# Keys and queries of an attention step transposed by VectorE and over DRAM instead of by TensorE

## What is computed

```python
z = h @ w_in
q, k, v, u, ga, gc = jnp.split(z, list(np.cumsum(IN_SPLITS)[:-1]), axis=-1)
o = moba_attention(to_heads(q), to_heads(k), to_heads(v))      # 16 heads of 128 channels
y_attn = o.transpose(0, 2, 1, 3).reshape(B, S, ATTN_WIDTH) @ w_attn_out
y_conv = conformer_conv(u, conv_dw, conv_db, conv_ln_g, conv_ln_b, w_conv_out)
merged = jax.nn.sigmoid(ga) * y_attn + jax.nn.sigmoid(gc) * y_conv
return merged @ w_out
```

## Time and profile before

| | us |
|---|---|
| median of 3 runs | 2117.32 (2117.18 to 2117.36) |
| the profiled execution | 2117.16 |
| its span in the trace | 2115.3 |
| TensorE busy | 2102.1 (99%) |
| VectorE busy | 1868.6 (88%) |
| ScalarE busy | 1406.2 (66%) |
| GpSimd busy | 194.2 (9%) |

### The profile page before, as it was taken

How to read it: one execution, slowest core, us unless ns; L and a number is a source line. 1 busy time by engine, 2 the same in 40 slices (tenths; PEclk the granted TensorE clock), 3 DMA queues, 4 the chain that set the end, 5 groups by cost and what they waited for, 6 DMA issues and landing times.

```text
span 2115.3 us, 23794 instructions
## 1 busy us (share of the span) xinstructions
PE 2102.1 (99%) x9420; PEld 1740.6 (82%) x9420; DVE 1868.6 (88%) x1404; ACT 1406.2 (66%) x1321; POOL 194.2 (9%) x305
## 2 busy tenths in 40 slices
PE   9999999999999999999999999999999999999998
PEld 7888888888888888888888888888888888888886
DVE  8899999999997889999899986659899999999996
ACT  6677777778775547666676435435677777777773
POOL 0111111100110000000000000000111111110110
PEclk9999999999999999999999999999999999999999
DMA  9688888898886759787888656755688888898883
GB/s 359 238 285 274 266 268 269 293 308 277 288 276 237 274 154 316 251 261 224 273 266 251 232 189 231 259 187 199 237 289 262 276 262 275 290 308 276 288 276 123
DMA packets 89709, 548.26 MB, mean 259 GB/s; under 512 B 12416, under 2 KB 12800, under 8 KB 32512
## 3 DMA queue, kind: packets, MB, share of 16 engines
q1 hardware_dynamic: 68544, 437.69, 54.5%
q0 software_dynamic: 21056, 109.07, 24.5%
HBM read 529.93 MB, written 16.78 MB: 258 GB/s over the span
## 4 chain that ended last, share of the span: by engine, by line
PE 99%; DMA 0%; DVE 0%; SPq 0%; ACT 0%; issue 0%; DVEq 0%
PE acc L2194 16%; PE acc L2196 16%; PE acc L2195 16%; PE tb L2194 12%; PE tb L2196 12%; PE tb L2195 12%; PE acc L2132 3%; PE acc L2134 3%; PE acc L2133 3%; PE tb L2180 1%; DMA g_raw<-in_groups 0%; PE tb L2475 0%; PE tb L2491 0%; PE tb L2492 0%; PE tb L2474 0%; DVE res L2035 0%
## 5 line engine op out<-in xcount | busy, mean ns | idle before, releaser
L1326 DVE TENSOR_TENSOR g_lo<-g_raw,g_hi 128x2048 fp32r<-128x2048 f32 x506 | 1147.3, 2285 | 136.5 <-ACT g_hi L804 136.1
L804 ACT ACTIVATE g_hi<-g_raw 128x2048 fp32r<-128x2048 f32 x506 | 964.7, 1916 | 343.3 <-DVE g_raw L1334 105.4
L2194 PE MATMUL acc<-g_hi,xF_hi 128*128 128x512 f32 x1216 | 477.9, 393 | 1.9 <-DVE g_lo L1653 1.3
L2196 PE MATMUL acc<-g_hi,xF_lo 128*128 128x512 f32 x1216 | 473.7, 390 | 0.0
L2195 PE MATMUL acc<-g_lo,xF_hi 128*128 128x512 f32 x1216 | 473.2, 389 | 0.0
L2194 PE MATMUL tb<-g_hi,xF_hi 128*128 128x512 f32 x760 | 297.1, 391 | 0.0
L2196 PE MATMUL tb<-g_hi,xF_lo 128*128 128x512 f32 x760 | 295.9, 389 | 0.0
L2195 PE MATMUL tb<-g_lo,xF_hi 128*128 128x512 f32 x760 | 295.7, 389 | 0.0
L1334 DVE TENSOR_TENSOR g_raw<-g_raw,g_raw 128x2048 f32<-128x2048 f32 x120 | 274.3, 2286 | 1.4
L2194 PEld LDWEIGHTS acc<-g_hi,xF_hi 128*128 128x128 f32 x1216 | 228.3, 188 | 50.3 <-DVE g_lo L1653 2.6
L2196 PEld LDWEIGHTS acc<-g_hi,xF_lo 128*128 128x128 f32 x1216 | 228.3, 188 | 48.2
(11 more groups left out here) (169 smaller groups left out, 2243.5 us busy)
## 6 DMA issues: line engine op xcount, KB each, us to landing
g_raw<-in_groups SPq DMA_DIRECT2D x356, 1024.0 KB, 7.0
g_raw<-in_groups POOLq DMA_DIRECT2D x80, 1024.0 KB, 8.3
raw<-in_stream SPq DMA_DIRECT2D x80, 512.0 KB, 4.7
bounce<-h_sq POOLq DMA_DIRECT2D x40, 256.0 KB, 5.0
h_in<-bounce POOLq DMA_DIRECT2D x160, 64.0 KB, 2.8
ln_gb<-in_ln SPq DMA_DIRECT2D x6, 1024.0 KB, 6.9
g_raw<-in_groups SPq DMA_DIRECT2D x6, 512.0 KB, 9.1
res<-in_x_rows SPq DMA_DIRECT2D x1, 2048.0 KB, 16.0
```

Of the source, the lines that this page charges most:

```text
L804: act.activation(g_hi[:, n % RING], source[:], ACT.Copy).then_inc(g_hi_ready, 1)
L1326: dve.tensor_tensor(g_lo[:, n % RING], source[:], f32(g_hi[:, n % RING]), ALU.subtract).then_inc(g_lo_ready, 1)
L2194: pe.matmul(bank, x_hi_ap, g_hi[:, n % RING, blk], start=begin, stop=False, skip_group_check=True)
L2196: return pe.matmul(bank, x_lo_ap, g_hi[:, n % RING, blk], start=False, stop=end, skip_group_check=True)
```

## The change

1. **Keys.** VectorE transposes `k_sb` in squares of 32 x 32 into `kT` (`keys_squared`, behind P1b's g_lo), GpSimd's queue writes `kT` to DRAM (`squares_out`), and ScalarE's own queue reads it back into `kT` in four pieces (`heads_in`), in its order ahead of P5a's split.
2. **Queries.** The same through `q_sq` and `q_bounce` (VectorE behind Q1's g_lo, ScalarE's reads ahead of P6a's split), and then ScalarE copies `q_sq` to `qT` behind P6a's split.
3. `turn_k`, `turn_q` and `heads_of` go. The **scores** of pair 0 stand behind P5b instead of Q2, those of pair 1 behind P6a instead of P5b. A head has three matmuls of 128 columns instead of one of 128 and one of 256, since `kT` holds the two halves of rows apart.
4. **Taps.** Ten counts per block: 0, 0, 0, 0, 2, 2, 3, 3, 3, 3 in the blocks with heads (16 as before; block 4 had 23), and 8 or 6 per gate group instead of 7 or 5.
5. **The first chunk.** 10 warm-up matmuls instead of 12; for each part of the first weights the matmuls with g_hi come first and wait for g_hi only, those with g_lo last.
6. **The first block** of the first network: the sum T3 is made by an accumulating DMA on GpSimd's queue (`t3_first`), and two `factor_lo` stand behind T1 instead of before the block.
7. `stats` lies elsewhere in SBUF, and the scratch for GpSimd's DMAs is 2048 instead of 1024.

```diff
-WARM = 12
+WARM = 10
-HALF_SUMS = ("T1", "T3", "T2", "T4")
+HALF_SUMS = (("T1", "T2", "T4"), ("T1", "T3", "T2", "T4"))
-BLOCK_TAPS = ((1, 3), (1, 3), (1, 3), (1, 3), (2, 3), (2, 1))
+HEAD_TAPS = (0, 0, 0, 0, 2, 2, 3, 3, 3, 3)
+BLOCK_TAPS = ((3, 3, 1, 1, 3, 1, 1, 1, 1, 1), *([HEAD_TAPS] * NG), (1, 1, 2, 2, 1, 2, 2, 2, 2, 2))
...
+    k_bounce = nc.dram_tensor("k_bounce", (QD, STEP, QD, TT, BLK, STEP), F32, kind="Internal").ap()
-        kT = mix("kT", [P, HG, T])
+        kT = mix("kT", [P, QD, TT, BLK, STEP])
+        q_sq = place("q_sq", [P, QD, TT, BLK, STEP], at=pr_at)
...
+            def heads_in(g, sent, dst, dram, loaded_all):
+                act.wait_ge(sent, 16 * (g + 1))
+                for c in range(QD):
+                    act.dma_start(dst[STEP * c:STEP * (c + 1)].rearrange("p a t b n -> p a (t b n)"),
+                                  dram[:, :, c].rearrange("a p t b n -> p a (t b n)")).then_inc(loaded_all, 16)
             def queries_turned(g):
+                act.wait_ge(q_loaded, 16 * QD * (g + 1))
                 if g:
                     act.wait_ge(o_stored, 16 * g)
-                heads_of(qT, g, 2)
+                for t in range(TT):
+                    act.activation(qT[:, :, t * P:(t + 1) * P].rearrange("p b (a n) -> p a b n", a=QD), q_sq[:, :, t],
+                                   ACT.Copy).then_inc(qT_ready, 1)
...
+            def square(dst, src, squared_one):
+                dve.transpose(dst.rearrange("p c b n -> p b c n"),
+                              src.rearrange("p (b c n) -> p b c n", b=BLK, c=QD)).then_inc(squared_one, 1)
...
+            def squares_out(g, squared_one, squares, dram, sent):
+                pool.wait_ge(squared_one, TT * (g + 1))
+                pool.dma_start(dram.rearrange("a p c t b n -> (a p) (c t b n)"),
+                               squares.rearrange("p c t b n -> p (c t b n)")).then_inc(sent, 16)
             def mixing_sums(g):
                 f = "mix"
+                if 0 < g <= NG:
+                    squares_out(g - 1, k_squared, kT[:], k_bounce, k_sent)
                 pool.wait_ge(g_lo_ready, lo_count(G.at[f, g, "P1b"]))
                 add_from_hbm(f, g, "qb", "rb", t1b_ready)
+                if 0 < g <= NG:
+                    squares_out(g - 1, q_squared, q_sq[:], q_bounce, q_sent)
...
+            pool.wait_ge(t_ready, G.sum_no[0, 1, "T1"])
+            add_from_hbm(0, 1, "ra", "ua", t3_first)
             round_trips(0)
...
                 for h in (2 * pair, 2 * pair + 1):
-                    pe.matmul(tb[:, h % 2, 0:P], qT[:, h, 0:P], kT[:, h, 0:P], start=True, stop=True)
-                    pe.matmul(tb[:, h % 2, P:SC], qT[:, h, P:T], kT[:, h, :], start=True, stop=True).then_inc(tr_full, 1)
+                    pe.matmul(tb[:, h % 2, 0:P], qT[:, h, 0:P], kT[:, :, 0, h], start=True, stop=True)
+                    pe.matmul(tb[:, h % 2, P:2 * P], qT[:, h, P:T], kT[:, :, 0, h], start=True, stop=True)
+                    pe.matmul(tb[:, h % 2, 2 * P:SC], qT[:, h, P:T], kT[:, :, 1, h], start=True,
+                              stop=True).then_inc(tr_full, 1)
```

More of the change, by code:

```diff
@@ L475, in build @@
         conv_step = sem("conv_step")
-        qk_ready = sem("qk_ready")
+        k_squared = sem("k_squared")
+        q_squared = sem("q_squared")
+        k_sent = sem("k_sent")
+        q_sent = sem("q_sent")
+        kT_loaded = sem("kT_loaded")
+        q_loaded = sem("q_loaded")
+        qT_ready = sem("qT_ready")
         s_ready = sem("s_ready")
@@ L1147, in mixing_block @@
                 if heads:
+                    heads_in(g - 1, q_sent, q_sq[:], q_bounce, q_loaded)
+                split_sum(f, g, "P6a", "qa", "T2a")
+                if heads:
                     queries_turned(g - 1)
-                split_sum(f, g, "P6a", "qa", "T2a")
                 split_loaded(f, g, "P3a", "ua")
@@ L1820, in mixing_block @@
                     conv_value(1)
-                taps(some)
+                if heads:
+                    queries_squared(g - 1)
+                taps(counts[0])
                 lo_group(f, g, "Q2", "Q2")
@@ L2253, in first_chunk @@
                     p = g // 2
-                    pe.wait_ge(part_lo, h + 1)
+                    pe.wait_ge(part_hi, h + 1)
+                    if h in (0, 4, 6):
+                        pe.wait_ge(x_hi, (0, 4, 6).index(h) + 1)
+                    for t in range(TT):
+                        for blk in range(first, last):
+                            high_only(banks[g % 2][t], piece(p, t)[0][:, blk], g, blk, p == 0 and blk == 0)
                     if h in (0, 4, 6):
```

123 lines of the change are left out of this document (66 added, 57 removed).

## The result

The changed kernel takes **2145.18 us** (median of 4 runs, 2143.3 to 2147.28) against 2117.27 for the kernel before beside it: ratio **1.0132**, 95% interval 1.0119 to 1.0144. It is 28 us slower, where 2110.1 (2108.0 to 2114.5) was forecast. Its profiled execution took 2146.07 us for a span of 2143.8.

The account below looks back on a forecast made before the run. TensorE, busy 99% of the span, was taken as the bound; 2117.16 - 1.28 (start) - 6.96 (transposes) + 1.2 (VectorE waits) = 2110.1 us, with a range of 2108.0 to 2114.5 for 8 in 10.

Parts of the forecast that it names:

- The way of the queries: Head blocks, queries through DRAM: qT ready at B + 16.5 to 20.5, wanted by TensorE at B + 21.8, so no wait.
- source of delay: Head blocks, DMA load: the squares add 2.1 MB per block, 31 GB/s, to 267 GB/s at a DMA share of 0.92.
- Rival (b): Head blocks: queries come late, ready at B + 27.3, a 5.5 us wait in each block, 2130.9 us; chance 0.08.
- Start, 1.28: Kernel start, fifth part of the first weights: matmuls begin at 12.35 instead of 13.63 us, a gain of 1.28 us.
- rival (c): First block: the start's gain is lost, VectorE late or P7 held by its DMA, 2111.4 us; chance 0.08.
- Transposes, 6.96: Blocks 1 to 4: turn_k and turn_q leave TensorE, eight pieces of 0.87 us, a gain of 6.96 us.
- Scores, 0: Scores in the head blocks: two 128-column matmuls instead of one of 256, operand in runs of 32 columns, cost 0.
- Rival (d): Scores: the moving operand lying in runs costs 10.5 us more, 2120.6 us; chance 0.03.
- VectorE, 1.2 us at P3b: Head blocks, pair 1's scores to P3b's g_lo: TensorE waits 0.3 us in each of four blocks, 1.2 us.
- Rival (a): Head blocks: VectorE becomes the bound, a block taking 68.1 instead of 66.75 us, time 2114.3 us; chance 0.13.
- Gates, 0: Gate groups: g_lo and eight taps take VectorE 5.5 us of TensorE's 5.44, entered over 4 us ahead: cost 0.
- What queues behind these waits: ScalarE in the head blocks: splits of P5a, P6a and P3a held by transfer waits, all covered by 2 us or more.

Follow-up runs that it names:

- first experiment: Kernel before with only the changed start (10 warm-ups, split first products, later factor_lo, T3 by accumulating DMA): 2116.13 us, ratio 0.9994.
- last run: Eighth experiment's kernel with seven convolution taps put back from the gate groups into block 4: 2112.3 us, ratio 0.9976.
- ninth run: Third experiment's kernel with both pairs of scores, and the steps that follow them, one product group later: 2136.07 us.
- fifth experiment: Third experiment's kernel with only the DRAM layout changed, so the one read DMA moves 1 KB rows instead of 4 KB: 2142.76 us.
- fourth experiment: Changed kernel, narrow rows kept, with GpSimd holding the sum T3b and those behind it until the query read lands: 2124.41 us, ratio 1.0031.
- sixth: Third experiment's kernel with the query write issued on ScalarE's queue behind P5a's split instead of GpSimd's: 2148.17 us.
- seventh: Sixth experiment's kernel with GpSimd also holding back T3b and what follows until the query read lands: 2129.36 us.
- third experiment: Changed kernel with the DRAM layout turned: four writes of 32 partitions in 1 KB pieces, one read with 4 KB rows: 2134.84 us, ratio 1.0085.
- second experiment: Changed kernel without the DMAs writing and reading the squares through DRAM, so scores are not the reference's: 2111.62 us, ratio 0.9971.
- eighth: Third experiment's kernel with only the keys going through DRAM and the queries turned on TensorE as before: 2114.14 us, ratio 0.9983.

## Why the prediction was wrong

**The step that failed is "The way of the queries"**: first its term for the query read, 3.5 us, and with it two terms that were given no time.

- *The read.* "64 KB took 2.8 us; I take 3.5 for 128 KB", with 7.0 as the far end. It took 6.3 to 9.6 us, and 17.8 in block 4. The 2.8 us of the earlier trace rows was a median over the whole kernel. With T3b held back the query read took 3 to 4 us, so 3.5 was its price with next to nothing else in flight; it was not the price in the first 25 us of a head block. It was the read and not the write: the query write landed at B + 13.6 to 15.8, at the late end of the forecast's B + 12 to 15, and with 3.5 us for the read qT would have been in time in three blocks and 0.3 us late in block 2. As it was, qT ended the wait in all four.
- *The keys.* I followed only their write ("lands by B + 2.7"; it landed at B + 3.3) and never costed their read, since 15 us seemed ample. It was the longest transfer, 18.4 to 19.2 us and 24.9 in block 4, and came after the scores were due in every block. It was hidden behind the later queries, and would have been the next wait.
- *Load as a "source of delay".* It was named and given no time. The 0.92 of the earlier trace rows is block 4's mean, and in the stretch in which the trip of block 2 must be done the share was lower still. What was missing is the trip's own engine time, added to that share. The page's part 3 for 897 to 920 before (B - 2.2 to B + 20.8) and for 901 to 926 after (B - 1.7 to B + 23.3), two windows with nearly the same sums and loads:

```profile
q0 software_dynamic: 305, 2.24, 54.2%
q1 hardware_dynamic: 288, 2.10, 22.2%
```

```profile
q0 software_dynamic: 576, 3.15, 55.4%
q1 hardware_dynamic: 288, 2.10, 21.3%
q10 hardware_dynamic: 1127, 1.03, 17.1%
```

Before: 76.4% of 23 us, 17.6 us of all 16 engines. After: 94% of 25 us, 23.5 us. So the trip costs some 6 us of every engine (an estimate from these rows), in a stretch that had 5 to 6 free and in which each transfer waits for another. In block 4 the same stretch was full already before: the share over 1034.4 to 1057.4 was 1.01 (such a share adds up packet times and can come out just above 1), against 0.79 over 899.24 to 922.24 in block 2. The trip had no room there, and the wait was 12.8 us.

**Rival (b) was the right mechanism.** It had 0.08. It had qT ready at B + 27.3, with reads of 7.0 us; in block 2 it was ready at B + 25.9, with reads of 6.3 to 7.3. It gave 5.5 us in each block, 2130.9. Blocks 1 to 3 waited about 4 each; what it lacked is block 4 (12.8) and the half clock behind every wait, 10.01 us in all. Its fault was the chance: the sum went by the kernel-wide median of the reads. The Trainium skill's rule that I cited (DMA: Bandwidth & Descriptors, "Issuing engines are not separate DMA queues") is borne out by the runs: ScalarE's query reads slowed with what GpSimd had in flight, from 3 to 4 us to 6 to 18. I had let it move only the query's read to 7.0 us.

**The other steps.**

- *Start, 1.28.* Right: the fifth part began at 12.19 instead of 13.63, and 1.39 us of it was left at the first head block. The first experiment shows that it differs between executions. No wait at u1, P5 or P7; rival (c) did not come.
- *Transposes, 6.96.* Right: 7.12.
- *Scores, 0.* Right: at full clock two heads take six matmuls of 0.22 us. Rival (d) fell.
- *VectorE, 1.2 us at P3b.* It cost nothing: 267.77 us of block and as much of busy TensorE without the trip. Rival (a) fell.
- *Gates, 0.* Wrong by 1.7 us. VectorE entered the gate groups ahead, as said, but left them late for sig_a. I looked whether the groups themselves were met, not at what stands behind them. In the profiled execution without the trip the stretch behind the blocks was 4.2 us longer than before (1021.79 against 1017.61), with 2.3 us of wait for sig_a and a granted clock of 0.79 just behind it (1224 to 1232). The last run took it back.
- *What queues behind these waits.* "All covered, by 2 us or more" rested on the query read. The ninth run shows the price: P3a's split stood behind it.

The sum without the failed step and without the 1.2 us that VectorE did not need, 2108.9, stands against 2111.62 of the kernel without the trip: the gates and the start that varies are the likely rest of 2.7 us, not told apart by a run.

What stays open: how the engines share themselves out between the queues. The fifth experiment shows a narrow read that is late while each of its packets costs no more than alone (elsewhere up to 68 ns of an engine were seen, with and without load), because few bytes go with each. Taking turns packet by packet with the long rows of the other queues (theory A) fits that, and so do the nearly equal packet counts of the three queues, but nothing here shows the turns themselves. Whether one queue serves its transfers strictly in order (theory C) stays open too. Nor was a trip tried on SyncE's queue.

## What to carry to other kernels

A transfer put on a timeline is priced with the DMA share and the queues of its own stretch plus what it adds itself, not with a median over the kernel. Where that stretch has 5 us of free engines in 25, a trip that needs 6 made something late in every order that was tried, and reordering only chose what. Cost every leg, also the one with ample time, and what stands behind each waiting instruction. Where several conditions release one instruction, compare the end of each with its start; the chain in the profile can name one that had long been met. Add to each wait of TensorE what its clock loses behind it: here 2.0 to 2.8 us a wait, for waits of 2.7 to 12.8 us. Taking half of the trip, the half that fits, beat both kernels.

## What the runs showed of the hardware

- A read of 512 KB took 18.8 us in 1 KB rows and 10.4 in 4 KB rows, with everything else alike, while the DMA share was 1.01 and 1.00. With next to nothing else in flight the query read took 3.0 to 4.0 us in narrow rows (medians of the four blocks, fourth experiment) and 3.1 to 3.3 in wide ones (sixth and seventh): the rows cost only under load.
- One megabyte of the accumulating sums takes over twice as much of the engines as one of plain loads (54.2% for 2.24 MB on q0, 22.2% for 2.10 MB on q1, before, in 23 us). Two such sums are most of the traffic of the stretch.
- After waits of 4.0, 4.1, 4.4 and 12.8 us TensorE ran at 1.2 GHz for 5.4, 3.6, 5.5 and 5.3 us (granted clock 0.57 from 1084 to 1090), which cost 2.0 to 2.8 us each. In the third experiment waits of 2.7 to 6.6 us cost 2.0 to 2.3 us each (both by the busy time of a block against the second experiment's). Behind the single waits of 1.3 us (eighth) and 1.5 us (kernel after) for sig_a the granted clock stayed 1.00.
